# Six extra matmuls on TensorE at the wait for the root, in each of nine norms of a two-block transformer kernel

## The reference, cut to what matters

```python
def rmsnorm(x, g):
    xf = x.astype(jnp.float32)
    y = xf * lax.rsqrt(jnp.mean(xf * xf, axis=-1, keepdims=True) + EPS)
    return (y * g.astype(jnp.float32)).astype(x.dtype)
...
def _layer_norm(x, g, b):
    xf = x.astype(jnp.float32)
    mu = jnp.mean(xf, -1, keepdims=True)
    var = jnp.mean(jnp.square(xf - mu), -1, keepdims=True)
    return ((xf - mu) * lax.rsqrt(var + LN_EPS) * g + b).astype(x.dtype)
```

## Time and profile before

| | |
|---|---|
| three runs | 1935.14, 1938.57, 1938.75 us; median 1938.57 |
| the profiled execution | 1932.61 us, of which 1930.8 us is the span from first to last instruction |
| PE, PEld busy | 94%, 91% |
| DVE, ACT, POOL busy | 55%, 49%, 20% |
| mean granted TensorE clock | 0.954 |
| the chain that ended last | PE 76%, DVE 8%, issue 5%, ACT 5%, POOL 3%, DMA 3% |

### The profile page before, as it was taken

One profiled execution on the slowest core, in us unless ns is written; L12 is line 12 of the kernel. 1 busy time (PEld: TensorE's weight loads), 2 busy tenths in 40 slices (PEclk: granted clock), 3 DMA queues, 4 the chain that ended last, 5 costly groups with the idle time before them and its releaser, 6 DMA issues.

```text
span 1930.8 us, 35099 instructions
## 1 busy us (share of the span) xinstructions
PE 1805.9 (94%) x15036; PEld 1748.6 (91%) x15036; DVE 1062.2 (55%) x1692; ACT 943.2 (49%) x1479; POOL 392.9 (20%) x281
## 2 busy tenths in 40 slices
PE   7899999999989999999999989889998999789997
PEld 7789999999988999999999879679998999789997
DVE  4355555775435665577645764345534667545433
ACT  5547745664445575566535431145523444445522
POOL 1200121341110002133204230134321000034320
PEclk9899999999989999999999989689999999879998
DMA  7324354545551434455464311015544333325540
GB/s 255 106 80 154 131 190 149 193 159 166 193 157 52 168 121 156 173 184 181 150 206 149 131 53 45 22 66 186 186 153 154 132 131 132 110 71 191 178 151 23
DMA packets 46139, 269.72 MB, mean 140 GB/s; under 512 B 4768, under 2 KB 8992, under 8 KB 19872
## 3 DMA queue, kind: packets, MB, share of 16 engines
q1 hardware_dynamic: 40752, 259.25, 39.2%
q10 hardware_dynamic: 5232, 8.23, 1.7%
HBM read 266.40 MB, written 1.05 MB: 139 GB/s over the span
## 4 chain that ended last, share of the span: by engine, by line
PE 76%; DVE 8%; issue 5%; ACT 5%; POOL 3%; DMA 3%; ACTq 0%; DVEq 0%; SPq 0%; POOLq 0%
PE b_ps L346 20%; PE b_ps L348 20%; PE b_ps L349 20%; PE b_ps L427 2%; DMA b_bias<-in_rpb 2%; PE b_ps L813 2%; DVE b_wlo L303 2%; ACT b_S L765 1%; PE b_ps L1693 1%; POOL b_mg L1203 1%; POOL b_bias L1195 1%; PE b_ps L792 1%; PE b_ps L396 1%; PE b_ps L395 1%; PE b_ps L394 1%
## 5 line engine op out<-in xcount | busy, mean ns | idle before, releaser
L346 PE MATMUL b_ps<-b_Hh,b_whi 128*128 128x256 f32 x2392 | 701.4, 293 | 21.2 <-ACT b_scr L548 7.4
L348 PE MATMUL b_ps<-b_Hl,b_whi 128*128 128x256 f32 x2392 | 689.1, 288 | 5.9 <-POOL b_Hl L562 3.6
L349 PE MATMUL b_ps<-b_Hh,b_wlo 128*128 128x256 f32 x2392 | 686.1, 287 | 0.0
L303 DVE TENSOR_TENSOR b_wlo<-b_wraw,b_whi 128x2048 fp32r<-128x2048 f32 (+3 forms) x276 | 566.9, 2055 | 173.1 <-PE b_ps L349 135.5
L295 ACT ACTIVATE b_whi<-b_wraw 128x2048 fp32r<-128x2048 f32 (+3 forms) x276 | 471.9, 1711 | 95.9 <-PE b_ps L349 81.4
L346 PEld LDWEIGHTS b_ps<-b_Hh,b_whi 128*128 128x128 f32 x2392 | 468.9, 196 | 32.4 <-issue 18.1
L348 PEld LDWEIGHTS b_ps<-b_Hl,b_whi 128*128 128x128 f32 x2392 | 468.8, 196 | 10.7 <-POOL b_Hl L562 4.2
L349 PEld LDWEIGHTS b_ps<-b_Hh,b_wlo 128*128 128x128 f32 x2392 | 468.7, 196 | 0.0
L348 PE MATMUL b_ps<-b_gl,b_whi 128*128 128x256 f32 x512 | 146.3, 286 | 0.0
L346 PE MATMUL b_ps<-b_gh,b_whi 128*128 128x256 f32 x512 | 146.1, 285 | 0.0
L349 PE MATMUL b_ps<-b_gh,b_wlo 128*128 128x256 f32 x512 | 146.0, 285 | 0.0
(11 more groups left out here) (335 smaller groups left out, 3085.8 us busy)
## 6 DMA issues: line engine op xcount, KB each, us to landing
b_wraw<-in_w SPq DMA_DIRECT2D x203, 1024.0 KB, 4.9
b_wraw<-in_w SPq DMA_DIRECT2D x32, 704.0 KB, 4.1
b_wraw<-in_w SPq DMA_DIRECT2D x33, 512.0 KB, 3.5
b_bias<-in_rpb ACTq DMA_DIRECT2D x8, 512.0 KB, 15.2
b_wraw<-in_w SPq DMA_DIRECT2D x2, 768.0 KB, 4.3
b_cA<-in_cA ACTq DMA_DIRECT2D x2, 608.0 KB, 6.4
b_X<-in_x SPq DMA_DIRECT2D x1, 1024.0 KB, 5.0
b_wraw<-in_w SPq DMA_DIRECT2D x4, 256.0 KB, 2.7
```

The source lines that it names most:

```text
L303: e.tensor_tensor(wlo[u % NLO][:, 0:n], raw[u % NRAW][:, 0:n], hi.bitcast(F32), ALU.subtract).then_inc(up("w_lo", "wlo", u))
L346: e.matmul(out, wh, x.hi[:, kk, :], start=k == 0, stop=False)
L348: e.matmul(out, wh, x.lo[:, kk, :], start=False, stop=False)
L349: ins = e.matmul(out, wl, x.hi[:, kk, :], start=False, stop=last)
```

## The change

`spread_pe` gets a parameter `fill`, and does so many plain fp32 matmuls (weights: the 128x128 ones; data: the first 256 columns of the constants) into columns 256 to 511 of the bank it has just taken, which no one reads, before it waits for the reciprocal. The nine norms of the residual pass 6; the four latent norms, and the offset spread of a layer norm, keep 0. In PE's order the six stand behind the last sum (L427) and ahead of the first spread. Nothing is moved or removed.

```diff
+FILL = 6
...
-    def spread_pe(e, w, c, key, need):
+    def spread_pe(e, w, c, key, need, fill=0):
         bank = banks.take(w, key)
+        for _ in range(fill):
+            e.matmul(bank[:, T:2 * T], ones, c1[:, 0:T], start=True, stop=True)
         w.wait_ge(*need)
...
-    def rms_pe(e, w):
+    def rms_pe(e, w, fill=0):
         i = w.next("norm")
-        spread_pe(e, w, 2, ("spread", i), at("rinv", i))
+        spread_pe(e, w, 2, ("spread", i), at("rinv", i), fill)
...
     def ln_pe(e, w):
         i = w.next("norm")
-        spread_pe(e, w, 2, ("spread", i), at("rinv", i))
+        spread_pe(e, w, 2, ("spread", i), at("rinv", i), FILL)
         spread_pe(e, w, 8, ("offset", i), at("mr", i))
...
-            rms_pe(e, w)
+            rms_pe(e, w, FILL)
```

## The result

| | before | changed |
|---|---|---|
| runs | 1931.86 to 1938.75 us, median 1936.86 (4 runs) | 1948.89 to 1954.32 us, median 1950.90 (4 runs) |
| ratio | | 1.0078, 95% interval 1.0052 to 1.0104 |
| profiled execution | 1932.61 us, span 1930.8 | 1949.69 us, span 1947.9 |
| mean granted clock | 0.954 | 0.962 |

The changed kernel is 14.0 us slower by the medians, and 0.78% by the ratio of the runs. TensorE's mean clock went up and the time with it. Lines stand one lower in the file up to the fillers and three lower behind them: the last sum is L428, a filler L440, a spread L443, `Hl` on POOL L496 and L565.

A forecast was written before the change was run, and what follows sets the result against it. PE was taken as the bound (busy 94%, 76% of the chain), with POOL's chunk 7 ending each norm. Rmsnorms 7.7 + layer norms 6.0 + first norm 1.3 - 0.4 = 14.6 us on median 1938.6 gave 1953 us, range 1944 to 1960.

The forecast's parts named there:

- The price of a filler: At each of nine norms: one plain fp32 128x256 matmul takes 0.43 us warm, so six take 2.58 us, or 5.2 cold.
- The rival of cheap fillers: All nine norms: fillers cost 0.11 us each and layer-norm spreads run warm; about 3.6 us faster, 1935 us; chance 0.04.
- The rmsnorms: Four rmsnorms after the first norm: 2.58 us of warm fillers in a 0.65 us hole, 1.93 us late each, 7.7 in all.
- the 0.4 that POOL's clearing gives back: Second mixer: with the norm later, POOL's buffer clearing is out of its way, an estimated return of 0.4 us.
- The layer norms: Four layer norms: delay between 0.1 and 3.7 us depending on the clock, taken as 1.5 each, 6.0 us in all.
- the case that I priced at 1.8: Layer norm: two fillers warm, four cold, clock back for the spreads; offset 1.8 us late, against 2.8 if not back.
- the case at 0.1: Layer norm: the clock stays up, fillers take 2.58 us, spreads 1.0 instead of 2.05; they end 0.1 us late.
- The first norm: First norm, 3.10 us hole at low clock: fillers overrun it, 0.7 to 2.1 us late, taken as 1.3 us.
- The step on which the sign hung: Behind each norm: POOL's low part of chunk 7 ends the job, so delaying the spread delays all and faster PE only waits.
- the clock pays: 48 matmuls behind each norm: PE ends the job, so a kept clock returns 12.4 us; net 4.0 faster, 1935 us; chance 0.08.
- Nothing absorbed: Rejects the rival that downstream waits, as on weight or bias transfers, absorb half the delay: +3 to +8 us, 1944; chance 0.08.

## Why the prediction was right

**The total.** 1953.0 was forecast from a median of 1938.6, 14.6 us more. Measured were 14.0 us, at 1950.9.

**The price of a filler.** 0.43 us warm was right (2.53 us from the last sum to the spread, for six). The rival of cheap fillers, 0.11 us each, is out. Fp32r matmuls do stand 0.11 us apart, and five of them as fillers left the spread where it was. The Trainium skill, "TensorE: Matmul & The Clock Gate", "Back-to-back issue gap", gives 109 ns for 256 columns as the gap of an isolated matmul, and its formula names no data type. By that formula, the fp32r rows agree and the plain fp32 rows, at four times as much, do not.

**The rmsnorms.** 1.93 us each was forecast, 1.8 measured, and 1.4 at the second mixer with the 0.4 that POOL's clearing gives back. The small rest is the spread itself, 0.61 us behind fillers and 0.68 behind idle time.

**The layer norms.** 6.0 in all was forecast, 5.4 in the profile (1.8, 1.7, 1.8, 0.1), which is the case that I priced at 1.8 (the clock falls and is back for the spreads) three times, and the case at 0.1 once. With fillers at the layer norms alone the last one cost 1.8 too. Which of the two comes at the last norm is the clock's doing, and differed between these two profiles. The term left something out, though. It took a kept clock to be worth nothing behind the norm; the rows show it to fall behind POOL's chunk 7 at both MLPs, for 1.5 us more each, and alone the layer norms cost 9.5 us (6.4 to 12.6), not 6.0.

**The first norm.** 1.3 was forecast, 0.9 measured: the fillers ended 1.5 us behind where the spread had started, the spread took 0.6 us less. The window prints a clock of 1.00 there, but six fillers took 4.6 us, so it was the low one most of the time; the profile has no record of it before 19.8 us. With fillers at the rmsnorms alone this norm cost 1.6 us, so the forecast lies between the two.

**Chunk 7.** The step on which the sign hung, that POOL's chunk 7 ends each norm, is shown at the feed-forward norms by the fp32r fillers (clock kept, PE idle 1.37 us, no gain) and by moving chunk 7 to DVE, after which a kept clock does gain. At the second mixer and RWKV the changed kernel itself shows it: the clock stays at 1.00 and PE stands idle for 1.4 us ahead of chunk 7. The rival "the clock pays" had its mechanism right and its condition wrong: at the first feed-forward PE and POOL were level, and 1.5 us of clock was worth nothing until POOL was out of the way.

**Nothing absorbed.** The norms' rows show 13.1 us and the runs 14.0; a second dose of six added 23 us more. My reason (the transfers are issued by engines behind the norm) was not tested apart.

**Luck in the sum.** Of the 14.6 us, 8.6 were forecast for the rmsnorms and 6.0 for the layer norms. Measured apart they are 5 (1 to 10) and 9.5 (6.4 to 12.6). The sum is closer than its parts are shown to be.

**What I did not foresee.** That the RWKV stage, untouched, differs by up to 10 us between profiles with the clock it gets. The range covered it by luck more than by a term.

## What to carry to other kernels

Filler matmuls keep the clock only for an engine that has something to do with it: look first at what ends the job behind the stall, and if it is another engine's chain, a faster PE only waits longer. Size fillers in the form that they really have (plain fp32 cost four times what fp32r did here) to the idle time in brackets, and put them where a wait is longest, not at the head of the chain that everybody waits for. Here the chain's last link had to be moved first (POOL's 2.8 us to 0.4 us on DVE); then two fillers behind the spread made the kernel 0.6 to 0.8% faster, while chunk 7 on DVE alone (0.9995) and two fillers behind the spread alone (0.9992) gave nothing. Look behind the next wait too: at the MLPs the clock fell behind it, where it cost. And do not take the norms' rows for the whole: fillers sized to the idle time gained 0.3% alone, and these rows do not say where.

## What the runs showed of the hardware

- Five fp32r matmuls, an estimated 0.55 us of work at 0.11 each, in a stall of 0.65 us kept the clock at 1.00 behind both feed-forward norms, but not behind the second mixer's and RWKV's (0.77). One plain fp32 matmul of 0.43 us kept it behind neither feed-forward norm (0.77). Two behind the spread, with chunk 7 on POOL, gave 0.82 behind the first of them and 1.00 behind the second and RWKV's; with chunk 7 on DVE, 1.00 behind both feed-forward norms, and the clock fell at RWKV's. One or two executions each; what decides there stays open.
- The same stage with the same 2679 PE records took 267.8 us at a mean clock of 0.87 and 275.1 at 0.84.
- POOL's subtraction of 128x256 takes 0.73 to 0.91 us beside DVE's operations on single chunks and 2.8 us while DVE splits a weight unit; moving one such operation took 2.4 us off the chain.
- With six or twelve fillers at the layer norms and chunk 7 on POOL, the clock fell behind PE's wait of 1.8 us for chunk 7 in all six MLP stages (a mean of 0.57 to 0.64 over 4 us); with fewer or none it did in three of twelve, and with chunk 7 on DVE, where PE does not wait there, in none of ten. A fall there made the stage some 1.5 us longer.
